# A Trainium2 kernel of two transformer layers: the convolution's input blocks turned on VectorE and through DRAM instead of on TensorE

## The chip, the core and the metric

The kernel is one program on one core of a Trainium2 chip. The metric is the device time of one execution in microseconds (us), the median of several. A core has TensorE (matmuls, whose results land in eight PSUM banks), VectorE (DVE), ScalarE (ACT), GpSimd (POOL) and SyncE (SP, which here issues nearly all DMAs), each with an instruction queue of its own that runs in order; they wait for each other on semaphores.

## The reference

Two transformer layers in sequence on an activation of 256 tokens by 1024 features, all in float32. The first has two kinds of attention and an MLP. The second has a gated FFN (ffn1), a mixing part (mix) and another gated FFN (ffn2). The change is in the mixing part, whose projection `z` is cut into the inputs of two branches; the first 1024 columns of `z` go through a causal convolution of width 4 over the tokens, channel by channel:

```python
u = rms_norm(x, mix_norm_g) * (1 + sc2) + sh2
z = u @ w_mix + b_mix
...
qk_m = jax.nn.silu(causal_conv(jnp.concatenate([q_m, k_m], axis=-1), conv_w, conv_b))
q_m, k_m = jnp.split(qk_m, 2, axis=-1)
h_m = mlstm_chunkwise(...)            # needs q_m and k_m of every channel
y_a = sigmoid(o_m) * rms_norm(h_m, mlstm_norm_g)
y_b = forgetting_attention(q_f, k_f, v_f, f_f, ...)   # "fox" in the kernel, 16 heads
merged = sigmoid(g_a) * (y_a @ w_branch_a) + sigmoid(g_b) * (y_b @ w_branch_b)
x = x + g2 * (merged @ w_out)
```

## The kernel before

**Matmuls.** Every projection is cut into blocks of 512 output columns (`conv0`, `conv1`, `vm0`, ...), a block into units of two k tiles of 128 rows, a unit into two halves, one for each row tile of 128 tokens. A raw float32 weight unit of 512 KB is loaded by SP (L2692), ScalarE rounds it to its high half `whi` (L1595), VectorE subtracts to get the low half `wlo` (L1983), and TensorE makes three float32r matmuls of 512 columns for each k tile and half: high by high, low by high, high by low (L1319, L1323, L1324). There are four raw buffers and five pairs of whi and wlo. SP loads the raw of a unit once the wlo of an earlier one has freed its buffer.

**The order.** A planner in Python (`plan`) writes one list, `order`, that all five engines walk through; each issues the entries that concern it. Everything besides the matmuls is a *job*: a generator with segments. After each half (and once more after each block) the planner ticks; a job whose lag has run down puts its next segment into the list, at most three jobs a tick. The lags between segments are the numbers of the table `LAG`, by kind and segment. Jobs take and drop buffers (`Ring`): four natural buffers `nat`, four PSUM banks `misc`, two convolution buffers `zp`, one `blocked_h` and one `land_h`. A `drain` ticks without halves until a job is done.

The blocks of the mixing part come as conv0, the small block gate, conv1, vm0, vm1, fox0 to fox3 (queries and keys of the fox attention), fv0, fv1, o0, o1, ga0, ga1, ba0 and on. conv0 ends at half 330 of the list, conv1 at 338, vm0 at 346, vm1 at 354, fox0 at 362, fox1 at 370, fox2 at 378, fox3 at 386, fv0 at 394, fv1 at 402, o0 at 410, o1 at 418, ga0 at 426.

**The convolution.** A block's two row tiles lie in PSUM with tokens on the partitions; the convolution wants channels there. ScalarE copies the tiles to `nat` (L1857). TensorE turns them by 128x128 transposes against an identity into a `misc` bank (L1518), four for each of two parts. ScalarE adds the bias and writes `zp` (L1868), VectorE makes the four taps into `qkT` (L2425, L2428), ScalarE applies Silu (L1875). In the list: the copy after half 330 (conv0) and 338 (conv1); conv0's four tap segments after halves 332, 338, 346 and 353, conv1's after 341, 347, 355 and 362; the last Silu after 359 and 368.

**What follows.** `mlstm` starts when conv0, conv1, vm0, vm1 and `gates` are done, here after half 377: for each of four heads one segment of scores (L1533) and two of sums (L1544 to L1547), with a VectorE normalisation each (L2477 to L2483) and a square on ScalarE (L1888); its last segment, the mean (L2488), stands after half 409. Behind block o0 the plan drains mlstm. Then SP loads `NF`, the forget terms of the fox attention (`load_nf`, L2808, two loads of 1 MB that wait for mlstm's last square and put), GpSimd masks them (L2627), and the first fox softmax (`fx0s`, L2205 on VectorE, L1754 on ScalarE) comes after half 418, ten ticks after fox3 is done and o0 has ended. The first turn of its results on TensorE (L1439) comes after half 423. The power on GpSimd that o0's normalisation (L2531) needs is L2594.

**The fox heads** already go the way that the change gives to the convolution: VectorE turns 32x32 blocks of two natural tiles into `blocked_h` (L2509), SP writes it to a DRAM scratch and reads it back into `land_h` in four pieces that put the blocks in place (`shuttle_heads`, L2731 and L2738), and ScalarE takes it from there (L1904). `land_h` has one buffer, so one block at a time is on this way.

Of the kernel before, what the change touches and what calls it, by code (L numbers as in the profile page):

```python
# [32 lines left out]
       ("attn_bw", 0): 2, ("attn_bw", 1): 6, ("attn_bw", 2): 1, ("attn_bw", 3): 24, ("conv", 0): 1, ("conv", 1): 2,  # L33
       ("conv", 2): 7, ("end", "late"): 6, ("end", "lead"): 4, ("ffn1", "between0"): 0, ("ffn1", "between1"): 0,
# [3 lines left out]
       ("fox", "fetch"): 6, ("fox", "put"): 4, ("gate", "ga0"): 15, ("gate", "ga1"): 24, ("gate", "gb0"): 8,  # L38
       ("gate", "gb1"): 11, ("fox", 0): 2, ("fox", 1): 5, ("fox", 2): 5, ("fx0", "wait"): 15, ("fx0s", "round"): 15,
# [8 lines left out]
       ("gates", 0): 11, ("gates", 1): 5, ("gates", 2): 20, ("gates", 3): 10, ("gates", 4): 6, ("glu", "fetch"): 4,  # L48
       ("glu", "upper"): 10, ("glu", "lower"): 0, ("glu", 0): 3, ("heads", "turn"): 3, ("heads", 0): 3,
       ("heads", 1): 3, ("heads", 2): 2, ("mT", "turn"): 0, ("mT", "wait"): 5, ("mix", "between0"): 0,  # L50
       ("mix", "between1"): 0, ("mix", "hold0"): 1, ("mix", "hold1"): 0, ("mix", "late"): 5, ("mix", "lead"): 5,
       ("mix", "turn0"): 3, ("mix", "turn1"): 2, ("mlp", "between0"): 0, ("mlp", "between1"): 0, ("mlp", "hold0"): 0,
       ("mlp", "hold1"): 0, ("mlp", "late"): 2, ("mlp", "turn0"): 3, ("mlp", "turn1"): 1, ("mlstm", 0): 4,
       ("mlstm", 1): 1, ("mlstm", 2): 4, ("o", 0): 1, ("o", 1): 5, ("o", 2): 18, ("pace", "gb0"): 4,
# [95 lines left out]
def build(nc, d, out):  # L150
# [3 lines left out]
    ACT = mybir.ActivationFunctionType  # L154
# [328 lines left out]
    def plan():  # L483
# [818 lines left out]
    def tensor_program(pe):  # L1302
# [207 lines left out]
        def conv_job(name):  # L1510
            yield
            for p in range(2):
                bank = misc.buf(name, p)
                pe.wait_ge(*misc.free(name, p))
                pe.wait_ge(*conv_in(name, 1))
                for c in range(2):
                    for t in range(2):
                        r = pe.e.transpose(bank[:, c * 256 + t * 128:c * 256 + t * 128 + 128],  # L1518
                                           nat.buf(name, t)[:, (2 * p + c) * 128:(2 * p + c + 1) * 128], ident[:, :])
                r.then_inc(turned.up(name, p), 1)  # L1520
                for _ in range(3):
                    yield
            for t in range(2):
                nat.give(turned(name, 1), name, t)
            yield

# [27 lines left out]
        def mT_job(c):  # L1554
# [6 lines left out]
                "conv0": conv_job("conv0"), "conv1": conv_job("conv1"), "mT0": mT_job(0), "mT1": mT_job(1)}  # L1561
# [28 lines left out]
    def scalar_program(act):  # L1590
# [262 lines left out]
        def conv_job(name, c0):  # L1853
# [6 lines left out]
            yield  # L1860
            for p in range(3):
                if p < 2:
                    z, bank = zp.buf(name, p), misc.buf(name, p)
                    act.wait_ge(*turned(name, p))
                    act.wait_ge(*zp.free(name, p))
                    act.wait_ge(*zero_zp(1))
                    for c in range(2):
                        r = act.e.activation(z[:, c, 3:259], bank[:, c * 256:(c + 1) * 256], ACT.Identity,  # L1868
                                             bias=col("bqk", c0 + 2 * p + c))
                    r.then_inc(conv_bias.up(name, p), 1)  # L1870
                    misc.give(conv_bias(name, p), name, p)
# [100 lines left out]
    def vector_program(dve):  # L1972
# [442 lines left out]

        def conv_job(name, c0):
            yield
# [73 lines left out]
        def fox_qk_job(name):  # L2491
# [12 lines left out]
            dve.wait_ge(*blocked_h.free(name))  # L2504
            dve.wait_ge(*gated("mix", 1, 1))
            o = blocked_h.buf(name)[:, :].rearrange("p (b t c j) -> p t b c j", b=4, t=2, c=4)
            for t in range(2):
                dve.wait_ge(*hn_out(name, t))
                v.transpose(o[:, t], bufs[t][:, :].rearrange("p (c b i) -> p b c i", c=4, b=4)).then_inc(  # L2509
                    swapped.up(name, t), 1)  # L2510
                nat.give(swapped(name, t), name, t)
# [171 lines left out]
    def sync_program(sp):  # L2683
# [41 lines left out]
        def shuttle_heads(name):  # L2725
            a = 262144
            for _ in range(3):
                yield
# [228 lines left out]
```

## Time and profile before

| | |
|---|---|
| time, median of 3 runs | 945.15 us (944.3 to 945.33) |
| time of the profiled execution | 944.73 us |
| its span | 943.4 us |
| TensorE busy | 935.1 us, 99% |
| VectorE busy | 718.6 us, 76% |
| ScalarE busy | 509.9 us, 54% |
| GpSimd busy | 50.1 us, 5% |
| DMA, mean over the span | 255 GB/s |
| TensorE's granted clock | 0.999 of full speed |

The span is that of the instructions in the trace; the time of the same execution is 1.3 us longer. Busy time of TensorE counts a matmul from its issue to its end, and matmuls overlap: of the 512 column matmuls a new one starts every 0.23 us though each lasts 0.39. What a piece of work costs TensorE is thus read from start times in a timeline and not from durations. A share of 76% for VectorE is a mean over the whole span; stretches stand higher.

### The profile page before, as it was taken

Reading aid. Unit: us, or ns where it says so; the run is one execution under the profiler, and the core shown is the slowest. Engines: PE = TensorE matmul, PEld = TensorE weight load, DVE = VectorE, ACT = ScalarE, POOL = GpSimd, SP = SyncE. Lnnn points to the kernel's source line nnn. Section 1 sums busy time; section 2 is a strip of 40 time slices with the busy share of each in tenths; the row PEclk is TensorE's granted clock in tenths of the full one; section 3 lists DMA queues with packets and bytes.
Section 4 is the critical chain, followed back from the end, with each engine's and each line's share of the span. In section 5 each row is a group of like instructions: output and inputs, shape, how many; then the busy total and the mean of one; then the engine's idle time right before and its main releaser. Section 6 shows DMA issues by size and latency. Waiting matters only on the chain.

```text
span 943.4 us, 12244 instructions
## 1 busy us (share of the span) xinstructions
PE 935.1 (99%) x4426; PEld 772.3 (82%) x4426; DVE 718.6 (76%) x1090; ACT 509.9 (54%) x792; POOL 50.1 (5%) x58
## 2 busy tenths in 40 slices
PE   9999999999999999999999999999999999999998
PEld 7878788888887888888888888878788888888886
DVE  6897689998676888777769999788666765566662
ACT  6686665564446445454576565456464574544440
POOL 2410000000000000000000121110000000000000
PEclk9999999999999999999999999999999999999999
DMA  9840779999894989998747889984735647666870
GB/s 341 266 152 23 246 245 372 389 387 371 286 317 148 332 326 343 320 345 299 274 133 259 279 281 283 302 338 147 234 125 188 213 137 264 225 223 223 300 234 23
DMA packets 123130, 240.31 MB, mean 255 GB/s; under 512 B 9346, under 2 KB 28954, under 8 KB 122814
## 3 DMA queue, kind: packets, MB, share of 16 engines
q1 hardware_dynamic: 122926, 239.27, 73.8%
q8 instruction: 35, 0.57, 0.2%
q10 hardware_dynamic: 144, 0.27, 0.1%
q14 instruction: 25, 0.20, 0.1%
HBM read 226.35 MB, written 14.20 MB: 255 GB/s over the span
## 4 chain that ended last, share of the span: by engine, by line
PE 87%; DVE 5%; DMA 5%; ACT 1%; issue 1%; SPq 1%; POOL 0%; DVEq 0%; ACTq 0%
PE ps L1319 27%; PE ps L1324 26%; PE ps L1323 26%; DMA raw<-in_w_mix 2%; DVE wlo L1983 2%; PE ps L1458 2%; PE ps L1414 1%; PE ps L1439 1%; PE ps L1350 1%; DMA land_h<-scr_u 1%; PE ps L1372 1%; ACT whi L1595 1%; DMA raw<-in_w_up 1%; DMA raw<-in_w_in 1%; PE ps L1571 1%
## 5 line engine op out<-in xcount | busy, mean ns | idle before, releaser
L1595 ACT ACTIVATE whi<-raw 128x1024 fp32r<-128x1024 f32 (+1 forms) x285 | 294.5, 1046 | 272.6 <-PE ps L1324 169.5
L1983 DVE TENSOR_TENSOR wlo<-raw,whi 128x1024 fp32r<-128x1024 f32 (+1 forms) x285 | 338.4, 1203 | 106.3 <-ACT whi L1595 105.8
L1319 PE MATMUL ps<-whi,hTh 128*128 128x512 f32 (+1 forms) x760 | 300.0, 395 | 0.2 <-DVE nat L2129 0.2
L1324 PE MATMUL ps<-whi,hTl 128*128 128x512 f32 (+1 forms) x760 | 294.4, 387 | 0.0
L1323 PE MATMUL ps<-wlo,hTh 128*128 128x512 f32 (+1 forms) x760 | 294.3, 387 | 0.0
L1319 PEld LDWEIGHTS ps<-whi,hTh 128*128 128x128 f32 x760 | 142.9, 188 | 30.8 <-issue 2.5
L1324 PEld LDWEIGHTS ps<-whi,hTl 128*128 128x128 f32 x760 | 142.7, 188 | 29.5
L1323 PEld LDWEIGHTS ps<-wlo,hTh 128*128 128x128 f32 x760 | 142.9, 188 | 27.8
L2325 DVE CUSTOM_DVE_ANT_0 araw<-araw,crow,colp 128x1024 f32<-128x1024 f32 x72 | 91.9, 1277 | 0.1
L2594 POOL TENSOR_TENSOR stat<-stat,mhalf 128x8 f32<-128x8 f32 (+3 forms) x29 | 36.2, 1260 | 586.0 <-DVE stat L1999 460.3
L1319 PE MATMUL ps<-whi,uh_ffn 128*128 128x512 f32 x164 | 63.9, 390 | 0.0
L1324 PE MATMUL ps<-whi,ul_ffn 128*128 128x512 f32 x164 | 63.8, 389 | 0.0
L1323 PE MATMUL ps<-wlo,uh_ffn 128*128 128x512 f32 x164 | 63.8, 389 | 0.0
L1319 PE MATMUL ps<-whi,uh 128*128 128x512 f32 x128 | 49.9, 390 | 0.0
L1323 PE MATMUL ps<-wlo,uh 128*128 128x512 f32 x128 | 49.8, 389 | 0.0
L1324 PE MATMUL ps<-whi,ul 128*128 128x512 f32 x128 | 49.8, 389 | 0.0
L2374 DVE TENSOR_TENSOR nat<-ps,nat 128x512 f32<-128x512 f32 (+1 forms) x24 | 15.4, 646 | 29.7 <-PE ps L1324 22.3
L1319 PEld LDWEIGHTS ps<-whi,uh_ffn 128*128 128x128 f32 x164 | 30.8, 188 | 6.4
L1324 PEld LDWEIGHTS ps<-whi,ul_ffn 128*128 128x128 f32 x164 | 30.8, 188 | 6.4
L1323 PEld LDWEIGHTS ps<-wlo,uh_ffn 128*128 128x128 f32 x164 | 30.8, 188 | 6.3
L1324 PEld LDWEIGHTS ps<-whi,ul 128*128 128x128 f32 x128 | 24.0, 188 | 5.0
L1323 PEld LDWEIGHTS ps<-wlo,uh 128*128 128x128 f32 x128 | 24.0, 188 | 5.0
(276 smaller groups left out, 1129.2 us busy)
## 6 DMA issues: line engine op xcount, KB each, us to landing
raw<-in_ffn_w_in SPq DMA_DIRECT2D x80, 512.0 KB, 5.1
araw<-in_w_mod SPq DMA_DIRECT2D x72, 512.0 KB, 5.6
raw<-in_w_mix SPq DMA_DIRECT2D x64, 512.0 KB, 4.9
raw<-in_ffn_w_out SPq DMA_DIRECT2D x44, 512.0 KB, 4.9
raw<-in_w_up SPq DMA_DIRECT2D x32, 512.0 KB, 5.4
raw<-in_w_down SPq DMA_DIRECT2D x32, 512.0 KB, 5.3
scr_u<-blocked SPq DMA_DIRECT2D x18, 512.0 KB, 5.0
raw<-in_w_out SPq DMA_DIRECT2D x16, 512.0 KB, 4.3
```

Source lines behind the costliest of these rows:

```text
L1319: pe.e.matmul(o, ah, h[:, j, :], start=s0, stop=False, skip_group_check=True)
L1323: pe.e.matmul(o, ah, l[:, j, :], start=False, stop=False, skip_group_check=True)
L1324: r = pe.e.matmul(o, al, h[:, j, :], start=False, stop=s1, skip_group_check=True)
L1350: r = pe.e.transpose(bank[:, c * 128:(c + 1) * 128], src[:, (4 * p + c) * 128:(4 * p + c + 1) * 128], ident[:, :])
L1372: r = pe.e.transpose(bank[:, c * 256 + t * 128:c * 256 + t * 128 + 128], src[t][:, (2 * p + c) * 128:(2 * p + c + 1) * 128], ident[:, :])
L1414: return pe.e.matmul(bank[:, c * w:(c + 1) * w], Q[rows, hp + c, ts], K[rows, kc(c), 0:w], start=True, stop=True)
L1458: r = pe.e.matmul(ob[:, h * 64:(h + 1) * 64], buf[:, (nk * c + k) * 128:(nk * c + k + 1) * 128], (fV if a["fox"] else VA)[:, k, v0:v0 + 64 ...
L1595: act.e.activation(uflat(whi, u), uflat(raw, u), ACT.Copy).then_inc(hi.up(u), 1)
L1983: v.tensor_tensor(uflat(wlo, u), uflat(raw, u), uflat(whi, u).bitcast(f32), SUB).then_inc(lo_dve.up(u), 1)
L2325: v.tensor_tensor_reduce(out=w, in0=w, in1=crow[:, :], scale=1.0, scalar=col("bada", 8 * m + i), op0=MUL, op1=ADD, accum_out=to).then_inc( ...
L2374: v.tensor_tensor(b[:, 0:n], pair_of(key)[t][:, c:512], b[:, 0:n], MUL).then_inc(glu.up(name, t), 1)
L2594: g.tensor_tensor(o, a, mhalf[:, 0:n], ALU.pow).then_inc(rstd.up(*key), 1)
```

## The change

In `job_conv` the planner no longer takes a `misc` bank; after the copy it waits until `blocked_h` and `land_h` are free, takes both, and has three new steps: the swap, the fetch (lag 6) and the put (lag 4). TensorE's `conv_job` is gone. VectorE makes the same block transposes as for the fox heads, by a helper `swap_heads` that both use. SP runs `shuttle_heads` for conv0 and conv1 too. ScalarE's bias activations read `land_h` instead of PSUM. The lags of several jobs are changed with it: conv 0 (1 to 2), fox fetch (6 to 4), fox put (4 to 6), fox 1 (5 to 9), fox 2 (5 to 1), fx0s wait (10 to 8), fx0s 0 to 3 (3, 4, 22, 2 to 11, 1, 14, 9), gates 1 (5 to 1), gates 3 (10 to 9), mlstm 2 (4 to 1), o 2 (18 to 15). All others stay.

```diff
@@ plan: job_conv
             yield lag("conv", 0, 2)
+            while None not in blocked_h.held or None not in land_h.held:
+                yield 1
+            blocked_h.take(name)
+            land_h.take(name)
+            seg(name)
+            blocked_h.drop(name)
+            natural_end(name)
+            yield lag("conv", "fetch", 6)
+            seg(name)
+            yield lag("conv", "put", 4)
             for p in range(2):
                 if p:
                     zp.drop(name, p - 1)
-                misc.take(name, p)
                 zp.take(name, p)
                 seg(name)
-                misc.drop(name, p)
+                if p:
+                    land_h.drop(name)
                 yield lag("conv", 1, 2)
...
             zp.drop(name, 1)
             seg(name)
-            natural_end(name)
@@ TensorE
-        def conv_job(name):
-            yield
-            for p in range(2):
-                bank = misc.buf(name, p)
-                pe.wait_ge(*misc.free(name, p))
-                pe.wait_ge(*conv_in(name, 1))
-                for c in range(2):
-                    for t in range(2):
-                        r = pe.e.transpose(bank[:, c * 256 + t * 128:c * 256 + t * 128 + 128],
-                                           nat.buf(name, t)[:, (2 * p + c) * 128:(2 * p + c + 1) * 128], ident[:, :])
-                r.then_inc(turned.up(name, p), 1)
...
@@ ScalarE: conv_job
+            view = land_h.buf(name)[:, :].rearrange("p (a t c j) -> p c t a j", a=4, t=2, c=4)
...
-                    z, bank = zp.buf(name, p), misc.buf(name, p)
-                    act.wait_ge(*turned(name, p))
+                    z = zp.buf(name, p)
+                    act.wait_ge(*ld_h(name, 3))
...
-                        r = act.e.activation(z[:, c, 3:259], bank[:, c * 256:(c + 1) * 256], ACT.Identity,
-                                             bias=col("bqk", c0 + 2 * p + c))
+                        r = act.e.activation(z[:, c, 3:259].rearrange("p (t a j) -> p t a j", t=2, a=4), view[:, 2 * p + c],
+                                             ACT.Identity, bias=col("bqk", c0 + 2 * p + c))
...
@@ VectorE
+        def swap_heads(name, ready):
+            dve.wait_ge(*blocked_h.free(name))
+            dve.wait_ge(*gated("mix", 1, 1))
+            o = blocked_h.buf(name)[:, :].rearrange("p (b t c j) -> p t b c j", b=4, t=2, c=4)
+            for t in range(2):
+                dve.wait_ge(*ready(name, t))
+                v.transpose(o[:, t], nat.buf(name, t)[:, :].rearrange("p (c b i) -> p b c i", c=4, b=4)).then_inc(
+                    swapped.up(name, t), 1)
+                nat.give(swapped(name, t), name, t)
+
         def conv_job(name, c0):
+            yield
+            swap_heads(name, conv_in)
+            yield
             yield
@@ SP
         def shuttle_heads(name):
             a = 262144
-            for _ in range(3):
+            for _ in range(1 if name[:4] == "conv" else 3):
                 yield
...
+        for c in range(2):
+            jobs[f"conv{c}"] = shuttle_heads(f"conv{c}")
```

## Rows read from the trace of the kernel before

**Rows 1.** The page: busy us, share of the span and instructions of each engine.

```profile
PE 935.1 (99%) x4426; PEld 772.3 (82%) x4426; DVE 718.6 (76%) x1090; ACT 509.9 (54%) x792; POOL 50.1 (5%) x58
```

**Rows 2.** Busy time by stretches of the span; last columns granted clock, DMA share, GB/s.

```profile
core 0: us, PE busy (x) PEld busy (x) DVE busy (x) ACT busy (x) POOL busy (x), PEclk, DMA share, GB/s
...
500.00:520.00 20.00, 20.00 (x95) 16.45 (x94) 19.02 (x30) 11.90 (x15) 1.41 (x2) 1.00 0.72 244
...
600.00:620.00 20.00, 20.00 (x92) 16.12 (x91) 16.46 (x27) 9.33 (x16) 3.72 (x2) 1.00 1.02 337
```

**Rows 3.** Timelines of VectorE and TensorE near 638 us: start, duration, engine, line.

```profile
636.24 2.10 DVE L1983 TENSOR_TENSOR wlo<-raw,whi 128x1024 fp32r<-128x1024 f32 x1
...
639.65 0.48 PE L1319 MATMUL ps<-whi,hTh 128*128 128x512 f32 x1
```

**Rows 4.** Timelines of TensorE and ScalarE near 625 us; in brackets idle time and releaser.

```profile
626.60 0.63 PE L1439 MATMUL ps<-ident,fP 128*128 128x128 f32 x4 [0.71 <-ACT fP L1754]
...
624.41 1.06 ACT L1595 ACTIVATE whi<-raw 128x1024 fp32r<-128x1024 f32 x1 [7.07 <-DMA raw<-in_w_mix]
```

**Rows 5.** Timeline of TensorE round the second group of transposes.

```profile
499.71 0.39 PE L1323 MATMUL ps<-wlo,hTh 128*128 128x512 f32 x1
499.94 0.40 PE L1324 MATMUL ps<-whi,hTl 128*128 128x512 f32 x1
500.18 0.60 PE L1518 MATMUL ps<-ident,nat 128*128 128x128 f32 x4
...
500.86 0.39 PE L1323 MATMUL ps<-wlo,hTh 128*128 128x512 f32 x1
```

**Rows 6.** The fox heads' landing buffer: ScalarE's waits and landings; then DMA issues.

```profile
  DMA land_h<-scr_u: 7.5, 3
...
DMA to landing us min/median/max: 3.9/6.0/7.4
...
scr_u<-gate SPq DMA_DIRECT2D x4, 512.0 KB, 3.4
```

**Rows 7.** VectorE: the fox transposes; timelines of three taps, of an mlstm normalisation.

```profile
L2509 DVE STREAM_TRANSPOSE gate<-nat x8: 665/684/706, 548.7 to 593.0; 128x512 f32<-128x512 f32 x8
...
498.43 1.53 DVE L2428 SCALAR_TENSOR_TENSOR qkT<-zp,colp,qkT 128x256 f32<-128x256 f32 x3
...
600.75 0.21 DVE L2477 TENSOR_SCALAR stat<-ps,emt 128x1 f32<-128x1 f32 x1
...
601.38 0.48 DVE L2483 TENSOR_SCALAR W<-ps,stat 128x256 f32<-128x256 f32 x1
```

**Rows 8.** Timeline of TensorE round one sum of mlstm.

```profile
558.65 0.59 PE L1544 MATMUL ps<-Vm,fP 128*128 128x257 f32 x2
558.89 0.58 PE L1319 MATMUL ps<-whi,hTh 128*128 128x512 f32 x1
```

**Rows 9.** conv1's last Silu on ScalarE, and TensorE's matmul behind half 368.

```profile
540.15 0.61 ACT L1875 ACTIVATE qkT<-qkT 128x512 f32<-128x512 f32 x1
...
541.64 0.39 PE L1319 MATMUL ps<-whi,hTh 128*128 128x512 f32 x1
```

**Rows 10.** The loads of NF, GpSimd's power and mask, and VectorE's wait for it.

```profile
L2808 SPq DMA_DIRECT2D NF<-scr_g x2: 419/428/437, 607.0 to 607.5; - x2
...
DMA to landing us min/median/max: 11.6/12.7/13.7
...
605.50 2.54 POOL L2594 TENSOR_TENSOR stat<-stat,mhalf 128x8 f32<-128x8 f32 x1 [26.93 <-DVE stat L2488]
618.83 2.09 POOL L2627 TENSOR_SCALAR_AFFINE_SELECT NF<-NF 128x1024 f32<-128x1024 f32 x1 [10.79 <-DMA NF<-scr_g]
...
621.06 0.42 DVE L2205 CUSTOM_DVE_ANT_0 fP<-ps,NF 128x256 f32<-128x256 f32 x1 [1.10 <-POOL NF L2627]
```

**Rows 11.** Timeline of TensorE: the first matmuls of o1 and of ga0's third unit.

```profile
606.76 0.39 PE L1319 MATMUL ps<-whi,hTh 128*128 128x512 f32 x1
...
624.37 0.39 PE L1319 MATMUL ps<-whi,hTh 128*128 128x512 f32 x1
```

More of the change, by code:

```diff
@@ L32 @@
        ("attn_bt", 0): 6, ("attn_bt", 1): 1, ("attn_bt", 2): 4, ("attn_bt", 3): 10, ("attn_bw", "round"): 10,
-       ("attn_bw", 0): 2, ("attn_bw", 1): 6, ("attn_bw", 2): 1, ("attn_bw", 3): 24, ("conv", 0): 1, ("conv", 1): 2,
+       ("attn_bw", 0): 2, ("attn_bw", 1): 6, ("attn_bw", 2): 1, ("attn_bw", 3): 24, ("conv", 0): 2, ("conv", 1): 2,
        ("conv", 2): 7, ("end", "late"): 6, ("end", "lead"): 4, ("ffn1", "between0"): 0, ("ffn1", "between1"): 0,
        ("ffn1", "hold0"): 0, ("ffn1", "hold1"): 0, ("ffn1", "late"): 3, ("ffn1", "lead"): 4, ("ffn1", "turn0"): 3,
[2 rows of a table removed]
@@ L38 @@
-       ("fox", "fetch"): 6, ("fox", "put"): 4, ("gate", "ga0"): 15, ("gate", "ga1"): 24, ("gate", "gb0"): 8,
-       ("gate", "gb1"): 11, ("fox", 0): 2, ("fox", 1): 5, ("fox", 2): 5, ("fx0", "wait"): 15, ("fx0s", "round"): 15,
[8 rows of a table removed]
-       ("gates", 0): 11, ("gates", 1): 5, ("gates", 2): 20, ("gates", 3): 10, ("gates", 4): 6, ("glu", "fetch"): 4,
-       ("glu", "upper"): 10, ("glu", "lower"): 0, ("glu", 0): 3, ("heads", "turn"): 3, ("heads", 0): 3,
-       ("heads", 1): 3, ("heads", 2): 2, ("mT", "turn"): 0, ("mT", "wait"): 5, ("mix", "between0"): 0,
@@ L51 @@
[L51 to L54, printed above, removed]
[2 rows of a table added]
+       ("fox", "turn"): 3, ("fox", "fetch"): 4, ("fox", "put"): 6, ("gate", "ga0"): 15, ("gate", "ga1"): 24,
@@ new lines @@
+       ("gate", "gb0"): 8, ("gate", "gb1"): 11, ("fox", 0): 2, ("fox", 1): 9, ("fox", 2): 1, ("fx0", "wait"): 15,
[8 rows of a table added]
+       ("fx1w", 6): 5, ("fx1w", 7): 1, ("gates", 0): 11, ("gates", 1): 1, ("gates", 2): 20, ("gates", 3): 9,
+       ("gates", 4): 6, ("glu", "fetch"): 4, ("glu", "upper"): 10, ("glu", "lower"): 0, ("glu", 0): 3,
+       ("heads", "turn"): 3, ("heads", 0): 3, ("heads", 1): 3, ("heads", 2): 2, ("mT", "turn"): 0, ("mT", "wait"): 5,
+       ("mix", "between0"): 0, ("mix", "between1"): 0, ("mix", "hold0"): 1, ("mix", "hold1"): 0, ("mix", "late"): 5,
@@ L55 @@
+       ("mix", "lead"): 5, ("mix", "turn0"): 3, ("mix", "turn1"): 2, ("mlp", "between0"): 0, ("mlp", "between1"): 0,
+       ("mlp", "hold0"): 0, ("mlp", "hold1"): 0, ("mlp", "late"): 2, ("mlp", "turn0"): 3, ("mlp", "turn1"): 1,
+       ("mlstm", 0): 4, ("mlstm", 1): 1, ("mlstm", 2): 1, ("o", 0): 1, ("o", 1): 5, ("o", 2): 15, ("pace", "gb0"): 4,
        ("pace", "gb1"): 9, ("pace", "kb"): 1, ("pace", "ob0"): 6, ("pace", "ob1"): 16, ("pace", "qa"): 11,
@@ L59 @@
        ("ta", "turn"): 1, ("ta", "wait"): 19, ("u", "fetch"): 6, ("u", "upper"): 10, ("u", "lower"): 1, ("u", 0): 3,
[1 row of a table removed]
+       ("vb", 0): 2, ("yT", "turn"): 24, ("yb", "turn"): 14, ("yb", "wait"): 9, ("conv", "fetch"): 6,
+       ("conv", "put"): 4}
 ROUNDS = (("soft", 0), ("soft", 1), ("mix", 0), ("soft", 2), ("mix", 1), ("soft", 3), ("mix", 2), ("mix", 3))
@@ L1508, in gates_job @@
                 yield
-        def conv_job(name):
-            yield
-            for p in range(2):
-                bank = misc.buf(name, p)
-                pe.wait_ge(*misc.free(name, p))
-                pe.wait_ge(*conv_in(name, 1))
-                for c in range(2):
-                    for t in range(2):
-                        r = pe.e.transpose(bank[:, c * 256 + t * 128:c * 256 + t * 128 + 128],
-                                           nat.buf(name, t)[:, (2 * p + c) * 128:(2 * p + c + 1) * 128], ident[:, :])
-                r.then_inc(turned.up(name, p), 1)
-                for _ in range(3):
[L1522 to L1525, printed above, removed]
         def mlstm():
@@ L1560, in tensor_program @@
                 "yb0": turns("yb0", 2, lambda t: yb_put(0, t)), "yb1": turns("yb1", 2, lambda t: yb_put(1, t)),
-                "conv0": conv_job("conv0"), "conv1": conv_job("conv1"), "mT0": mT_job(0), "mT1": mT_job(1)}
+                "mT0": mT_job(0), "mT1": mT_job(1)}
         for name in ("qb", "kb"):
@@ L1867, in conv_job @@
                     for c in range(2):
-                        r = act.e.activation(z[:, c, 3:259], bank[:, c * 256:(c + 1) * 256], ACT.Identity,
-                                             bias=col("bqk", c0 + 2 * p + c))
+                        r = act.e.activation(z[:, c, 3:259].rearrange("p (t a j) -> p t a j", t=2, a=4), view[:, 2 * p + c],
+                                             ACT.Identity, bias=col("bqk", c0 + 2 * p + c))
                     r.then_inc(conv_bias.up(name, p), 1)
-                    misc.give(conv_bias(name, p), name, p)
+                    if p:
+                        land_h.give(conv_bias(name, p), name)
                 if p:
@@ L2414, in gates_job @@
                 yield
+        def swap_heads(name, ready):
[7 more added lines that the diff above has]
+                nat.give(swapped(name, t), name, t)
         def conv_job(name, c0):
+            yield
+            swap_heads(name, conv_in)
+            yield
             yield
@@ L2503, in fox_qk_job @@
             yield
[L2504 to L2511, printed above, removed]
+            swap_heads(name, hn_out)
             yield
@@ L2726, in shuttle_heads @@
             a = 262144
-            for _ in range(3):
+            for _ in range(1 if name[:4] == "conv" else 3):
                 yield
```

21 rows, old and new, of the table LAG are left out of this document.

## The prediction

> **What bounds the kernel.** I read the page's busy times first: TensorE shows 935.1 us of a 943.4 us span [rows 1], so the time is TensorE's, and the table of stretches shows it busy without a break from 480 to 620 us, where the changed work lies [rows 2]. The same table shows VectorE at 19.02 of 20 us there and the DMA engines at 0.72 to 1.02: whatever leaves TensorE goes to two resources with little left. The kernel gains only what leaves TensorE, and loses wherever VectorE hands over a weight's low half (wlo) later than TensorE wants it. That margin is small at places: one wlo ends at 638.34 and its first matmul starts at 639.65 [rows 3]. From 500 to 700 us the one plain wait of TensorE is 0.71 us at 626.60, for ScalarE [rows 4].
>
> **What is removed.** Sixteen transposes in four groups of four. In the timeline [rows 5] the matmul before a group starts at 499.94 and the second matmul behind it at 500.86: 0.92 us where two ordinary steps take 2 x 0.227 (499.71 to 499.94 is one). A group therefore costs 0.47 us: its issue and about 0.09 us on the first matmul behind it. Four make 1.9 us (1.7 if the group that the small gate transposes follow saves less, since those stay). The row gives 0.60 us from the first start to the last end of a group; 4 x 0.60 = 2.4 us is the upper bound, which the start times exclude, since the next matmul begins before the last one ends. The Trainium skill (VectorE: DVE Perf Modes, Rules for kernel authors) speaks against the change: for a full 128x128 transpose use TensorE if a PSUM destination is fine, since VectorE turns 32x32 blocks only. By its table of bf16 transposes (390 ns on TensorE) the 16 would be an estimated 6.2 us; the rows give 1.9.
>
> ScalarE's eight bias activations read SBUF instead of PSUM: nothing, since ScalarE has slack (11.90 busy of 20 us).
>
> **What is added.** Four VectorE block transposes of 684 ns [rows 7], 2.7 us, and two trips through DRAM: one 512 KB write and four 128 KB reads each, 10 DMA issues on SP's queue, 2 MB in all. For the fox heads the write lands in 3.4 us and a read in 3.9 to 7.4 [rows 6]. Nothing on TensorE waits for the trips themselves: the next reader is ScalarE, and behind it in its queue are the whi conversions, which now and then wait up to about 3 us more for a landing, as they did for the fox heads (7.5 us in three waits [rows 6], with no gap on TensorE). SP waits for the swap with raw loads queued behind, but for the same VectorE that those loads wait for.
>
> The 2.7 us on VectorE are covered by what is moved. The order counts a tick after each half (two k tiles of one row tile, 12 matmuls a unit of two halves, 2.74 us) and one more after each block. By LAG, conv0's swap comes at half 331, its taps at 341, 347, 355 and 361 (before: 332, 338, 346, 353). There is one landing buffer, so conv1 cannot swap until conv0 gives it up at half 354; its taps come at 365, 371, 379 and 385, and it ends at half 392 instead of 368. A tap segment is 1.9 us: three taps of 1.53 us together behind a first one [rows 7]. VectorE's work done up to a given half is thus below before until about half 400, by up to 5 us. The gate scans come one tick before TensorE's gate transposes instead of five; by the relieved VectorE queue they still end some 1 us earlier: priced at 0 (up to 1 us without that relief).
>
> **What is late next.** mlstm starts when conv1 is done: half 392, not 377. With the lag 4 cut to 1 it takes 24 ticks instead of 36, and the plan drains it behind block o0 (half 410). It used to end at 409; now its last four ticks fall into the drain, where no half lies between them. Three consequences.
>
> First, three float32 groups of TensorE stand side by side. A lone one costs the first matmul behind it extra time: behind the one at 558.65, of 0.24 us, the next matmul shows 0.58 us instead of 0.39 [rows 8]. Two such edges in the drain, and one where a double tick joins two groups, are worth about 0.4 us (0 to 0.6).
>
> Second, mlstm's first scores follow conv1's last Silu in the same tick. Before, that Silu ended at 540.76 and TensorE came to its place at 541.64 [rows 9]. I add 0.4 us (0 if it is as early again, 1.5 if ScalarE sits in a DMA wait).
>
> Third, the loads of NF (the forget terms) wait on SP for mlstm's last squares. Call P the time at which TensorE starts block o1; before, it was 606.76, and NF was issued at 607.0, landed in 11.6 us, and GpSimd's mask ended at 620.92, P + 14.2 [rows 10]. The first fox softmax on VectorE needs the mask and waited 1.10 us for it. Now at P come the last two steps on VectorE (two times 1.1 us [rows 7]), ScalarE's square and the mean, with hand-overs some 3.8 us: NF goes out at P + 3.8. With the same queueing the mask ends at P + 17.4; with an emptier queue (a landing of 7 us, which is the longest of a 0.1 MB read) at P + 12.8. And the softmax is placed earlier: fox3 is done at tick 95, the lag is 8 instead of 10, so it stands at half 416 and not 418, ahead of the wlo of the third unit of ga0. VectorE is in order: softmax 1.5 us, the two steps of o0 (1.3 us) and that wlo (1.2 us) follow the mask, so the wlo ends between P + 16.8 and P + 21.4. TensorE wants it at 624.37, P + 17.6 [rows 11]. Stall: 0 to 3.8 us. The power on GpSimd (2.54 us) also moves from before P to P + 6.3 [rows 10], o0's normalisation waits for it, and the wlo behind that ends near P + 9.2 where it is wanted at P + 8.2: about 1 us, part of the same loss. I take 2.3 us for both, nearer the middle, since the DMA engines are full there (1.02 [rows 2]).
>
> In return the 0.71 us wait of rows 4 goes: it came because the exponentials stood behind a whi that waited 7.07 us for its raw, and two halves earlier they stand ahead of it. The margin between that softmax and the first turn grows from five halves to seven.
>
> **Sum.** Against the profiled execution's own 944.73 us (span 943.4 and 1.3 around it): -1.9 - 0.4 - 0.7 + 0.4 + 2.3 = -0.3, so 944.4. The median of the runs shown is 945.15, 0.4 above the profiled one; I forecast 944.5. A measurement of this kernel tells about 0.2% (1.9 us) from no change.
>
> **The rivals.**
> - *Same* (forecast, 0.42): the removed 3.0 us are mostly given back at the NF wait. 943.3 to 946.9; its own range 943.4 to 946.4.
> - *The full gain* (0.30): NF lands early, or VectorE comes to the softmax late anyway, as with the 1.10 us before. Then 944.73 - 3.0 + 0 to 1.1 = 941.7 to 942.8 in the profiled time, 942.2 to 943.2 as a median. For it: TensorE has not one wait in 500 to 620 us, so every removed cycle counts. Against it: the placement of the softmax, which the lags fix.
> - *VectorE becomes the bound behind the late mlstm* (slower, 0.20): place, halves 410 to 420; the mask at P + 17.4, and the weights behind it (each later raw waits on SP for an earlier wlo, and lands after 5 us or, as the one that ScalarE waited 7.07 us for, much later) miss their time too. It decides once the wlo end more than 5 us late. 944.73 - 3.0 + 6 to 7 = 947.7 to 948.7; with a softmax turn caught as well, 949.
> - *The landing is the loss* (slower, 0.08): a read of conv's blocks lands late in the busy DMA (7.4 us and more), and ScalarE holds back the whi behind it for longer than margins like that of rows 3 allow, once for each of the two blocks, 2 to 3 us each: 944.7 - 3.0 + 5 = 946.7 to 947.5.
> - That the transposes were hidden and nothing is saved: the start times of rows 5 exclude it.
>
> **Range and chances.** No gain beyond 3.0 us exists, so 942.2 is the floor; the upper end takes in the first 1.5 us of the slower cases: 942.2 to 947.5 leaves out about 2 in 10. Faster by over 0.2%: 0.30, within: 0.42, slower: 0.28.
>
> **What would show it.** In the profile after: no L1518 groups, first matmuls of blocks spaced 0.23 us at those places; L2509's line in its helper with 12 instead of 8 transposes; a wait of VectorE's softmax on GpSimd's NF mask of 3 to 5 us instead of 1.10; a gap on TensorE at the third unit of ga0 behind wlo, and perhaps at the fourth of o1; no wait on fP at the first fox turn; a short wait at mlstm's first scores. I am wrong if the NF wait is no longer than before (full gain) or if TensorE has gaps between halves 340 and 390 (the trips or the queue of VectorE cost something there).

## The result and the profile after

The changed kernel takes 950.86 us (median of 4 runs, 949.63 to 952.36) against 945.24 for the kernel before (4 runs, 944.3 to 945.79): ratio 1.0057, 95% interval 1.0035 to 1.0079. It is slower by 5.6 us, outside the forecast range. The profiled execution took 952.36 us, the longest of the four, with a span of 951.0 us, 7.6 above that of before, so the balance below is that of a run 1.5 us over the median.

The page's busy times after, to be laid beside [rows 1]:

```profile
PE 935.6 (98%) x4410; PEld 770.4 (81%) x4410; DVE 720.2 (76%) x1094; ACT 514.6 (54%) x795; POOL 48.3 (5%) x58
```

Sixteen matmul instructions fewer, and TensorE's busy time is no smaller. The stretches show where the idle time came in (columns as in [rows 2]):

```profile
500.00:520.00 20.00, 20.00 (x92) 16.33 (x91) 14.32 (x23) 7.91 (x10) 1.42 (x2) 1.00 0.79 251
520.00:540.00 20.00, 20.00 (x90) 16.57 (x89) 19.04 (x29) 11.04 (x13) 1.23 (x1) 1.00 1.00 327
540.00:560.00 20.00, 17.13 (x75) 13.58 (x74) 17.54 (x27) 18.52 (x27) 5.37 (x4) 1.00 0.68 224
560.00:580.00 20.00, 16.94 (x73) 13.05 (x71) 19.72 (x33) 11.44 (x17) 3.41 (x2) 1.00 0.95 310
580.00:600.00 20.00, 19.30 (x81) 16.07 (x82) 19.01 (x35) 8.76 (x17) 3.33 (x2) 0.91 0.89 281
```

From 500 to 520 us VectorE is busy for 14.32 us where it had 19.02 [rows 2]. Behind that, TensorE loses about 6.6 us between 540 and 600. Its timeline gives the gaps, each with its length and releaser in brackets:

```profile
545.43 0.47 PE L1329 MATMUL ps<-whi,hTh 128*128 128x512 f32 x1 [2.41 <-DVE wlo L1980]
557.05 0.47 PE L1329 MATMUL ps<-whi,hTh 128*128 128x512 f32 x1 [0.46 <-DVE wlo L1980]
565.84 0.50 PE L1329 MATMUL ps<-whi,hTh 128*128 128x512 f32 x1 [0.36 <-DVE wlo L1980]
569.87 0.47 PE L1329 MATMUL ps<-whi,hTh 128*128 128x512 f32 x1 [0.99 <-DVE wlo L1980]
580.70 0.67 PE L1526 MATMUL ps<-qkT 128*128 128x256 f32 x2 [2.40 <-ACT qkT L1872]
```

Four gaps are waits for a weight's low half, 4.2 us; the fifth is mlstm's first scores behind conv1's last Silu, 2.40 us. Right behind the fifth the granted clock falls to half, as a window laid on that place shows, and the starts of the matmuls move from 0.23 us apart to 0.43:

```profile
581.40:584.80 3.40, 3.40 (x10) 2.71 (x9) 3.40 (x4) 1.06 (x1) 2.63 (x2) 0.50 0.53 156
585.00:590.00 5.00, 5.00 (x24) 4.17 (x23) 4.81 (x10) 2.13 (x5) 0.00 (x0) 1.00 1.07 329
```

```profile
582.75 0.63 PE L1329 MATMUL ps<-whi,hTh 128*128 128x512 f32 x1
583.17 0.63 PE L1333 MATMUL ps<-wlo,hTh 128*128 128x512 f32 x1
...
585.08 0.39 PE L1329 MATMUL ps<-whi,hTh 128*128 128x512 f32 x1
585.31 0.39 PE L1333 MATMUL ps<-wlo,hTh 128*128 128x512 f32 x1
```

That stretch at the 1.2 GHz level lasts 3.4 us and costs half of it, 1.7 us. The balance of the profiled run: gaps +6.6, clock +1.7, transposes -1.9, the wait of rows 4 -0.7, and 0.4 that was there before the first conv: +6.1 of 7.6. The other 1.5 us are spread over the float32 groups that moved and the first matmuls behind gaps, and I give them to no row.

The 2.41 us gap can be followed back. First ScalarE, then VectorE:

```profile
541.23 0.91 ACT L1864 ACTIVATE zp<-land_h,colp 128x256 f32<-128x256 f32 x2 [2.86 <-DMA land_h<-scr_u]
```

```profile
542.17 0.41 DVE L2435 TENSOR_SCALAR qkT<-zp,colp 128x256 f32<-128x256 f32 x1 [2.69 <-ACT zp L1864]
542.62 1.53 DVE L2438 SCALAR_TENSOR_TENSOR qkT<-zp,colp,qkT 128x256 f32<-128x256 f32 x3
544.07 2.36 DVE L1980 TENSOR_TENSOR wlo<-raw,whi 128x1024 fp32r<-128x1024 f32 x2
```

conv1's block lands late, ScalarE waits for it, VectorE stands with its taps for 2.69 us, and the wlo behind the taps come late to TensorE. The trace has a second, earlier chain. SP's DMA issues (start, time of the issue), then ScalarE:

```profile
497.00 2.68 SPq L2741 DMA_DIRECT2D land_h<-scr_u  x4
499.72 0.43 SPq L2695 DMA_DIRECT2D raw<-in_w_mix  x1
...
501.99 0.31 SPq L2798 DMA_DIRECT2D scr_g<-F  x1
509.34 0.38 SPq L2800 DMA_DIRECT2D EM<-scr_g  x1
...
510.32 1.01 SPq L2695 DMA_DIRECT2D raw<-in_w_mix  x2
```

```profile
506.36 0.91 ACT L1864 ACTIVATE zp<-land_h,colp 128x256 f32<-128x256 f32 x2 [5.83 <-DMA land_h<-scr_u]
...
517.49 1.06 ACT L1588 ACTIVATE whi<-raw 128x1024 fp32r<-128x1024 f32 x1 [5.85 <-DMA raw<-in_w_mix]
```

The 20 KB store of the gate rows goes out at 501.99, behind conv0's reads. SP waits 7.0 us for it before it may read those rows back, with the raw loads queued behind; before, the same wait was 1.6 us. Not all of the growth is the trip's: with the new lags alone (e2_lags below) the wait is 3.1 us. The Trainium skill (DMA: Bandwidth & Descriptors, Anatomy of one DMA — SWDGE (gpsimd) path) gives a DMA on GpSimd's path a fixed cost of about 2.0 us. This store is issued by SP; its wait of before is near that figure, and that of after is far over it. These two chains, VectorE's load, the lags, and the single landing buffer were then set against each other.

### The profile page after: what moved, and what is told of

It is laid out like the page before. It is cut to its first block, busy times and chain, and to the rows that moved or that the text cites. A ratio compares the mean times of both kernels' runs of the same rounds, so it can differ in the third digit from the quotient of the medians.

```text
span 951.0 us, 12233 instructions
## 1 busy us (share of the span) xinstructions
PE 935.6 (98%) x4410; PEld 770.4 (81%) x4410; DVE 720.2 (76%) x1094; ACT 514.6 (54%) x795; POOL 48.3 (5%) x58
## 4 chain that ended last, share of the span: by engine, by line
PE 85%; DVE 7%; DMA 4%; ACT 2%; issue 2%; SPq 0%; POOL 0%; DVEq 0%; ACTq 0%
PE ps L1329 26%; PE ps L1333 26%; PE ps L1334 26%; DVE wlo L1980 3%; PE ps L1468 2%; DMA land_h<-scr_u 1%; ACT whi L1588 1%; PE ps L1424 1%; PE ps L1382 1%; PE ps L1449 1%; DMA raw<-in_w_mix 1%; PE ps L1360 1%; DVE araw L2322 1%; DMA raw<-in_w_up 1%; DMA raw<-in_ffn_w_in 1%
## 5 line engine op out<-in xcount | busy, mean ns | idle before, releaser
L2597 POOL TENSOR_TENSOR stat<-stat,mhalf 128x8 f32<-128x8 f32 (+3 forms) x29 | 34.1, 1188 | 594.4 <-DVE stat L1996 461.0
L1329 PEld LDWEIGHTS ps<-whi,uh 128*128 128x128 f32 x128 | 24.0, 188 | 5.0
```

What stands on the lines that cost most here:

```text
L1329: pe.e.matmul(o, ah, h[:, j, :], start=s0, stop=False, skip_group_check=True)
L2597: g.tensor_tensor(o, a, mhalf[:, 0:n], ALU.pow).then_inc(rstd.up(*key), 1)
```

## The experiments

Each kernel's ratio is to the kernel before in the same series of runs. Fourteen kernels were run. A ratio has an interval of 0.1 to 0.2% to each side, 1 us or more, and several steps below are no larger. So a second measure stands beside it. Every trace holds the same 3696 matmuls of 512 columns, and from the start of the 1801st to that of the 2521st (in the kernel before from 460.69 to 651.13 us) each covers the changed work and leaves out what varies ahead of it; behind this piece no two of the kernels below drift apart by more than 0.1 us. What a kernel takes there beyond the kernel before is called its *excess* below; it comes from one execution each and has no interval. For the changed kernel it is 7.2 us, 1.7 of it the half clock.

**e1_notrans.** The kernel before without TensorE's transposes; ScalarE reads natural instead of turned blocks, which leaves the transposition out of the result.

```diff
-                "conv0": conv_job("conv0"), "conv1": conv_job("conv1"), "mT0": mT_job(0), "mT1": mT_job(1)}
+                "mT0": mT_job(0), "mT1": mT_job(1)}
...
-                    act.wait_ge(*turned(name, p))
+                    act.wait_ge(*conv_in(name, 1))
```

> The kernel before, with the sixteen transposes on TensorE left out: ScalarE's bias activations read the natural tiles as they are, so the convolution runs on untransposed data (that part of the computation is changed). Nothing else moves. It measures the price of the transposes by itself. By the start times of the timeline they are worth 1.9 us: 943.3 us, ratio 0.998. If their whole durations counted it would be 4.4 us: 940.8. If they were hidden: 945.2.

Measured: 942.73 us, ratio 0.9982 (0.9972 to 0.9991), so -1.7 us. The first term of the forecast, 1.9, stands: over the transposes the trace gains 1.9 us. Its excess is -2.6, since the 0.71 us wait of [rows 4] is gone here too, although no lag was changed.

**e2_lags.** The kernel before with the new lags of all other jobs (fox, fx0s, gates, mlstm, o).

```diff
+LAG.update({('fox', 'fetch'): 4, ('fox', 'put'): 6, ('fox', 1): 9, ('fox', 2): 1, ('fx0s', 'wait'): 8,
...
```

> The kernel before, transposes on TensorE and all, with the changed lags of fox, fx0s, gates, mlstm and o alone (conv's own lag stays at 1). If the loss of 5.6 us comes from the landing way (one buffer, late landings, mlstm late), this one stays within 1.5 us of before, 943.7 to 946.7. If it comes from the retuned lags of the other jobs, it is as slow as the changed kernel: 948 to 951.

Measured: 945.37 us, ratio 1.0005 (0.9996 to 1.0014). The lags alone cost nothing that can be told (excess -0.15).

**e3_two.** The changed kernel with a second blocked buffer, landing buffer and DRAM block for conv1, and the lags of the other jobs as before, so that conv1 need not wait for conv0.

```diff
-    blocked_h = Ring([gates[0]])
+    blocked_h, blocked_c = Ring([gates[0]]), Ring([gates[1]])
+    land_c = Ring([W1[:, 1, :]])
```

> The changed kernel with a second way for conv1: its blocks go into the other gate row's tile, through a DRAM slot of their own and land in the upper half of W1, so that conv1 need not wait for conv0's landing buffer. All lags of the other jobs as before the change; conv's are 2, fetch 4, put 6, last 6, so that conv1's last Silu stands after half 374 and mlstm starts at 377 as before. If the single landing buffer and what it makes late is the cause, the 1.9 us of the transposes are kept: 943.0 to 944.0. If the cause is VectorE's 2.7 us of swaps, or the trips as such, it stays slow: 948 to 951.

Measured: 955.3 us, ratio 1.011 (1.0095 to 1.0124): by the ratios 5 us worse than the changed kernel. TensorE's waits:

```profile
PE ps L1533 <- ACT qkT L1880: 4.2, 1, 4.2
PE ps L1336 <- DVE wlo L1988: 2.6, 3, 1.1
```

A second landing buffer does not bring the gain back. Since the two trips and the taps also stand closer together here, and the waits are more, this run does not price the buffer by itself.

**e4_noland.** The changed kernel, but conv's bias activations read a weight tile (W1) and wait for no landing; swaps and trips are all done.

```diff
-            view = land_h.buf(name)[:, :].rearrange("p (a t c j) -> p c t a j", a=4, t=2, c=4)
+            view = W1[:, 0, :].rearrange("p (a t c j) -> p c t a j", a=4, t=2, c=4)
...
-                    act.wait_ge(*ld_h(name, 3))
```

> The changed kernel with swaps, writes and reads in their places, but ScalarE's bias activations of the convolution read a tile that is already there (a half of W1) and so wait for no landing; the convolution's data are changed by it. If ScalarE's wait for conv1's landing is what holds VectorE's taps and the wlo behind them, the gap of 2.41 us at 545 us and those behind it go, with the wait of 2.40 us for the last Silu left: 946 to 948.5. If VectorE is simply overfull, nothing changes: 950 to 951.

Measured: 948.14 us, ratio 1.0038 (1.0026 to 1.0051). TensorE's waits in its trace:

```profile
PE ps L1526 <- ACT qkT L1871: 2.4, 1, 2.4
PE ps L1329 <- DVE wlo L1979: 2.3, 4, 1.0
```

The long gap of 2.41 us is gone, but four waits for wlo stay and most of the loss with them. The landing wait is worth 1.8 us by the ratios (their intervals overlap), about a third. By the excesses, 7.2 and 3.3, it is 3.9, of which 1.7 are the half clock that this execution did not have.

**e5_gatewait.** The changed kernel with SP's wait for the gate rows' store and the loads behind it a segment later.

```diff
+LAG.update({('gates', 1): 6, ('gates', 2): 15})
...
             q.dma_start(scrG[4:24, :], F8[:, :]).then_inc(st_gates.up(1), 16)
+            yield
             sp.wait_ge(*st_gates(1))
```

> The changed kernel; on SP the wait for the landing of the gate rows in DRAM, and the two EM loads behind it, stand one segment later (lags gates 1 = 6, gates 2 = 15, so that the later gate segments keep their places). In the changed kernel SP stood 7.0 us in that wait with raw loads queued behind it, 1.6 us before the change. If that queueing is a main cause, VectorE gets its raws earlier and the wlo waits of TensorE (4.2 us in four) shrink: 947 to 949. If it is not: 950 to 951.

Measured: 949.82 us, ratio 1.0058 (1.0045 to 1.0071); TensorE waits 2.4 us in 4 for wlo and 2.4 for the Silu. The wlo waits shrink by 1.8 us as forecast, the time does not: with the landing wait in place the stand of SP makes no difference in it that can be told. The excess, 5.2, is 2.0 better, but it is one execution.

**e6_spread.** The changed kernel with the landing given more time (lag put 8 instead of 4), conv's last lag shortened, and mlstm at its old place.

```diff
+LAG.update({('conv', 'put'): 8, ('conv', 2): 5})
...
+            yield 4
```

> The changed kernel with conv's put lag 8 instead of 4 and its last lag 5 instead of 7: ScalarE asks for a landing four ticks later, the buffer is given up at the same tick as before, the last Silu of conv1 stands four ticks earlier, and mlstm still starts at its old place. ScalarE's waits for the two landings (8.7 us) and TensorE's 2.40 us wait for the Silu should go; the SP wait stays. Theory landing and Silu: 945.5 to 947.5. Theory VectorE overfull: the wlo waits stay, 948.5 to 950.

Measured: 952.84 us, ratio 1.0091 (1.0078 to 1.0104). ScalarE waits for no landing of conv; wlo are late for 4.9 us in 4 waits, up to 2.4. More time for the landing does not help. That this is so because the taps move further into a stretch where VectorE is full fits the wlo waits, but was not tested.

**e7_both.** The edits of e5_gatewait and e6_spread together:

```diff
+LAG.update({('gates', 1): 6, ('gates', 2): 15, ('conv', 'put'): 8, ('conv', 2): 5})
...
+            yield 4
...
+            yield
             sp.wait_ge(*st_gates(1))
```

> The two edits together: SP's wait one segment later, landings asked for later, Silu four ticks ahead of mlstm. If waits in line (landing, SP, Silu) are the whole loss, the gain of the transposes comes out: 943 to 944.5. What stays above that is the price of VectorE's 2.7 us of swaps and of the late mlstm: 945 to 948.

Measured: 948.93 us, ratio 1.0052 (1.004 to 1.0064): 3.9 us better than e6_spread. So here SP's stand did cost; wlo still 3.8 us in 4.

**e8_silu.** The changed kernel with mlstm two ticks later, so that TensorE would not meet the Silu:

```diff
+            yield 2
```

> The changed kernel with mlstm two ticks later behind conv1's last Silu, nothing else. TensorE's wait of 2.40 us there should go, and the half clock behind it, if that comes from the gap. Theory Silu: 947 to 949. If the time is only moved to the late end of mlstm (VectorE and SP behind it): 950 to 951.

Measured: 952.69 us, ratio 1.0085 (1.0071 to 1.0098). The Silu wait is gone and wlo come late for 7.1 us in 7 waits, up to 3.2. So the 2.4 us cannot simply be subtracted: where this edit takes them away, as much or more is paid elsewhere. The edit also makes mlstm later still, and which of the two brings the new waits stays open.

**e9_noswap and e10_empty.** From e4_noland first VectorE's swaps are taken away (the trips carry the buffer as it is), then the trips too. What stays of the change in e10_empty is the places and the missing transposes.

```diff
-            swap_heads(name, conv_in)
+            for t in range(2):
+                nat.give(conv_in(name, t), name, t)
```

```diff
-        for c in range(2):
-            jobs[f"conv{c}"] = shuttle_heads(f"conv{c}")
```

> The version without the landing wait (e4_noland), with VectorE's four swaps of the convolution's blocks left out as well: the DMA trips stay and carry the buffer as it is. VectorE is given back 2.7 us, 1.3 of it between 540 and 560 us. Theory VectorE is too full there: the waits of TensorE's matmuls for wlo (four, up to 2.3 us in e4_noland) shrink to under 1 us in all and the median is 945 to 946.3 us. Theory the cost is where the work stands or what the DMA queues carry, not the swaps: 947.5 to 948.5 us, as e4_noland (948.14).

> As e9_noswap, and the DMA trips of the convolution are left out too: what is left of the change is that the 16 TensorE transposes are gone and that the convolution's and the mLSTM's pieces stand at their new places. Beside e1_notrans (942.73, same pieces at the old places) it prices the places alone. Theory places cost (taps moved into a full stretch): at least 944.5 us, 2 us or more over e1_notrans. Theory swaps and trips are the whole cost: 942.5 to 943.5 us. What the trips themselves cost is its difference from e9_noswap; if the queues do not matter, under 0.5 us.

Measured: e9_noswap 947.47 us, ratio 1.0033 (1.002 to 1.0045); e10_empty 944.39 us, ratio 0.9998 (0.9989 to 1.0006). I had expected the large step at the swaps. By the ratios it is at the trips, whose landing nothing on ScalarE waits for in either kernel: without swaps the time is that of e4_noland within the interval; without trips it falls by 3.1 us, and there the intervals are apart. The excesses (e4_noland 3.3, e9_noswap 1.6, e10_empty 0.0) give the trips 1.6 and the swaps 1.7. Both measures say that the trips cost something; only the ratios say that they cost more than the swaps. The chain shows in the waits of SP and ScalarE and in VectorE's timeline, first of e9_noswap:

```profile
SPq L2800 <- DMA scr_g<-F: 6.5, 1, 6.5
```

```profile
516.67 1.06 ACT L1588 ACTIVATE whi<-raw 128x1024 fp32r<-128x1024 f32 x1 [6.65 <-DMA raw<-in_w_mix]
```

```profile
517.77 2.50 DVE L1979 TENSOR_TENSOR wlo<-raw,whi 128x1024 fp32r<-128x1024 f32 x2 [3.11 <-ACT whi L1588]
```

and of e10_empty, SP and ScalarE at the same places:

```profile
SPq L2800 <- DMA scr_g<-F: 3.1, 1, 3.1
```

```profile
511.25 1.06 ACT L1588 ACTIVATE whi<-raw 128x1024 fp32r<-128x1024 f32 x1 [3.62 <-DMA raw<-in_w_mix]
```

With the trips the raws land late, and VectorE stands idle for 3.11 us with wlo, right ahead of the 20 us from 520 us in which it has under one to spare. TensorE's waits in e10_empty are smaller:

```profile
PE ps L1526 <- ACT qkT L1871: 1.6, 1, 1.6
...
PE ps L1329 <- DVE wlo L1979: 0.4, 1, 0.4
```

The profiled spans are 945.9 and 942.6. Of the 3.3 us between them 1.6 arise ahead of the first conv, where the kernels do the same; 1.6 are the waits of the Silu (2.4 against 1.6) and of wlo (1.2 against 0.4). The medians, 3.1 apart over 12 runs each, hold a part that the profiled pair lacks: in 10 of e9_noswap's 12 runs the mean granted clock was under 1.000 (0.996 to 0.999), in e10_empty's 6 of 12 (all 0.999), in e2_lags' none of 11. The two e9_noswap runs at 1.000 average 945.3 us and the six at 0.998 948.3. A run at 0.998 has lost about 0.002 x 946 = 1.9 us to the clock, about as much as the piece at half clock at 581 us above. Over all 12 runs the mean clock is 0.9984 against 0.9995, an estimated 1.0 of the 3.1 us. So about a third of what the trips cost by the ratios is granted clock; that the trips' waits bring this about is not shown.

Beside e1_notrans (0.9982) e10_empty prices the places and, with them, the new lags of the other jobs: +1.5 us, less than the 2 that I had put to it; the intervals overlap by 0.0002, and e2_lags gave 0.5 for the lags alone (its interval takes in 0). By the excesses it is 2.6. In the trace 2.0 of them are two waits of TensorE: 1.6 for conv1's last Silu and 0.4 for a wlo.

**e11_half.** The kernel before with conv0 alone sent by swaps and trip, the swap put where VectorE had been idle, conv1 turned by TensorE.

```diff
+            far = name == "conv0"
...
+                if not far:
+                    misc.take(name, p)
...
+        jobs["conv0"] = shuttle_heads("conv0")
```

> Only conv0's block goes by VectorE's swaps and the DRAM trip, placed where VectorE stood idle before the gate matmuls; conv1's block is turned by TensorE as before, and every other job keeps its place. TensorE saves 8 transposes (0.9 us). Theory VectorE room: the stretch from 520 us on is left alone, no wlo wait over 1 us appears, and the median is 943.3 to 944.2 us, a little faster than before. Theory any trip costs more than the transposes: 945.5 us or more.

Measured: 944.7 us, ratio 0.9999 (0.9989 to 1.0008). No wait for wlo and a full VectorE:

```profile
500.00:520.00 20.00, 20.00 (x94) 16.36 (x93) 19.07 (x31) 12.23 (x17) 1.42 (x2) 1.00 0.84 287
520.00:540.00 20.00, 20.00 (x92) 16.55 (x91) 19.50 (x35) 10.45 (x14) 0.80 (x1) 1.00 0.82 265
```

Placed so, a trip makes no wlo late, but the 0.9 us that its 8 transposes should give is not seen in the time (the excess, -0.6, has it in part), and the result is neither of my two ranges. No version of the idea that was run beats the kernel before.

**e12_landgate, e13_trip1, e14_trip0.** How do the trips cost 3 us? e12_landgate is e4_noland with the edit of e5_gatewait:

```diff
+LAG.update({('gates', 1): 6, ('gates', 2): 15})
...
+            yield
             sp.wait_ge(*st_gates(1))
```

The other two are e9_noswap with one trip each:

```diff
-        for c in range(2):
-            jobs[f"conv{c}"] = shuttle_heads(f"conv{c}")
+        jobs["conv1"] = shuttle_heads("conv1")
```

(`conv0` for e14_trip0).

> The version without the landing wait (e4_noland: the bias activations read W1 instead of the landed block), and in it the gate jobs' pieces one segment later as in e5_gatewait, so that SP does not stand for the gate rows' tiny store with raw loads behind it. Theory the trips cost because SP stands 7 us behind them: 945 to 946.3 us, no ScalarE wait for a raw load over 4 us between 500 and 520 us. Theory the trips cost by what they carry on the queue, or the places cost: 947.5 to 948.5 us, as e4_noland (948.14).

> As e9_noswap (no swaps by VectorE, bias activations read W1), and conv0's DMA trip is left out, so that only conv1's is left. e9_noswap with both trips took 3.1 us more than e10_empty with none (947.47 against 944.39). Theory the first trip is the cost, as it stands right ahead of the gate rows' store and the raw loads of 500 to 520 us: 944.4 to 945.2 us. Theory each trip costs the same: about 945.9 us. Theory the second is the cost (it meets the stretch where VectorE is full): 946.8 to 947.5 us.

> The other half of e13_trip1: conv1's DMA trip is left out and conv0's is left. Theory the first trip is the cost: 946.8 to 947.5 us, with SP's wait for the gate rows' store at 6 us or more and a ScalarE wait for a raw load over 5 us, as in e9_noswap. Theory each trip costs the same: about 945.9 us. Theory the second is the cost: 944.4 to 945.2 us.

Measured: e12_landgate 946.92 us, ratio 1.0022 (1.0012 to 1.0033); e13_trip1, with conv1's trip, 944.92, ratio 1.0 (0.9989 to 1.0012); e14_trip0, with conv0's, 946.61, ratio 1.0013 (1.0005 to 1.0022). SP's wait and ScalarE's longest wait with the first trip alone (e14_trip0):

```profile
SPq L2800 <- DMA scr_g<-F: 5.9, 1, 5.9
```

```profile
517.01 1.06 ACT L1588 ACTIVATE whi<-raw 128x1024 fp32r<-128x1024 f32 x1 [7.06 <-DMA raw<-in_w_mix]
```

and with the second alone (e13_trip1):

```profile
SPq L2800 <- DMA scr_g<-F: 2.8, 1, 2.8
```

```profile
512.24 1.06 ACT L1588 ACTIVATE whi<-raw 128x1024 fp32r<-128x1024 f32 x1 [3.78 <-DMA raw<-in_w_mix]
```

The first trip makes the gate rows' store and the raws late, and the second does not; that much the rows show. What each costs is not shown. By the ratios the first costs 1.4 us, the second alone 0.2 and both 3.3, but the intervals of the two single trips overlap (1.0005 to 1.0022, 0.9989 to 1.0012). Their traces do not part them: the excesses are 0.8 and 0.7, about the 1.6 of both together, and TensorE's waits are the same in each, 2.4 us for the Silu and 0.4 for one wlo. In e14_trip0 7 of 11 runs had a mean clock of 0.998, in e13_trip1 4 of 12 were at 0.998 or lower; the runs at 1.000 average 945.3 and 944.7 us. So by the traces SP's stand is not the only way in which a trip costs: the second has its excess of 0.7 us without it. Taking the stand away gives back 1.5 us (e12_landgate against e4_noland), with intervals that overlap by 0.0007.

## Why the prediction was wrong

The ladder of ratios, from the kernel before at 1:

| kernel | ratio | what it adds to the one above | us | excess, and its step |
|---|---|---|---|---|
| e1_notrans | 0.9982 | transposes gone | -1.7 | -2.6, -2.6 |
| e10_empty | 0.9998 | the new places and lags | +1.5 | 0.0, +2.6 |
| e9_noswap | 1.0033 | the DMA trips | +3.3 | 1.6, +1.6 |
| e4_noland | 1.0038 | VectorE's four swaps | +0.5 | 3.3, +1.7 |
| changed | 1.0057 | ScalarE's wait for the landing | +1.8 | 7.2, +3.9 (1.7 of it clock) |

Steps need not add up in another order. Of the last four only the step of the trips has intervals that are apart, and the two measures rank the four differently, so which part is the largest stays open. That the four together turn a gain of 1.7 us into a loss of 5.4 is shown.

**The step that failed** is "Nothing on TensorE waits for the trips themselves". I looked at who reads the landed block and at SP's wait for the swap, and left out what the ten new issues do to the transfers queued behind them. In e9_noswap no computing engine waits for the trips, and yet they cost 3.3 us by the ratios (about 1.0 of it clock), 1.6 in the traces. What the traces show of the way: conv0's trip stands ahead of raws and of a 20 KB store on which SP waits; that store kept SP for 5.7 to 7.2 us instead of 2.8 to 3.1 with the new lags and no conv0 trip, and the raws behind it, then whi, then wlo came late. How conv1's trip costs was not followed. I had the parts: the landing times of [rows 6] and the DMA share of [rows 2]. ScalarE's wait for the landing was priced at nothing in the sum, at up to 3 us without a gap; it was 5.83 and 2.86 us, the second with a gap of 2.41 us. The rival "the landing is the loss" had this second mechanism with 0.08; by e4_noland it is 1.8 of 5.6 us, with intervals that overlap.

**The second failed step** is that "VectorE's work done up to a given half is thus below before until about half 400", read as cover. The places were right: the taps come at halves 341 to 361 and 365 to 385, as worked out from LAG. But work that is later is not room gained. What VectorE did not do from 500 to 520 us became idle time (5.7 us of it), since wlo cannot be made ahead of its raw; the taps then met 20 us in which it already worked 19.6, as the row of the kernel before shows:

```profile
520.00:540.00 20.00, 20.00 (x91) 16.54 (x91) 19.61 (x32) 12.30 (x15) 1.62 (x2) 1.00 0.86 297
```

The +1.5 of e10_empty fits this only in part: from 560 to 580 us its VectorE works 19.8 of 20 us, but of TensorE's waits there 1.6 us are for the Silu and 0.4 for a wlo. That this lost time on VectorE is what made the trips' lateness cost is argued, not shown.

**The Silu term** had the right place and the wrong size: 0.4 (0 to 1.5) against 2.40 in the trace. In e10_empty, without swaps, trips and landing wait, it is still 1.6, so most of it comes with the new places: there the Silu stands on ScalarE behind squares that waited 1.17 us for VectorE and two whi. By e8_silu it cannot be taken away by moving mlstm alone.

**The NF term** of 2.3 us, which decided the forecast, did not come. NF went out at 616.9, landed in 7.8 to 10.1 us, and the mask (1.10 us from 624.82) was done 2.2 us ahead of VectorE's first softmax:

```profile
617.12 1.64 POOL L2597 TENSOR_TENSOR stat<-stat,mhalf 128x8 f32<-128x8 f32 x1 [33.09 <-DVE stat L2498]
624.82 1.10 POOL L2630 TENSOR_SCALAR_AFFINE_SELECT NF<-NF 128x1024 f32<-128x1024 f32 x1 [6.06 <-DMA NF<-scr_g]
```

```profile
628.13 0.41 DVE L2202 CUSTOM_DVE_ANT_0 fP<-ps,NF 128x256 f32<-128x256 f32 x1
```

Block o1 starts at P = 614.6 here, so the mask ended at P + 11.3 (forecast P + 12.8 to P + 17.4). VectorE, late itself, came after it, and behind 580.70 us the trace shows no wait of TensorE up to 700. The saving of 0.4 us for float32 groups that stand together was measured by no run.

**Right** were the 1.9 us of the transposes (1.7) and the end of the wait of [rows 4], though the reason given was not needed for it: the wait is gone in e1_notrans as well, where the exponentials keep their place in the list. The swaps, held to be covered, cost 0.5 us by the ratios, within the interval, and 1.7 by the excesses: not settled. The rival of a VectorE that becomes the bound names a resource that is part of it and had the time nearest to the measured one (947.7 to 948.7, or 949), but placed it behind mlstm at halves 410 to 420; the gaps lie at halves 371 to 393. The prediction's own test, gaps between halves 340 and 390, named the failure.

## What to carry to other kernels

Before a transfer is added, list what is queued behind it on its DMA queue, above all small stores that the issuing engine waits for, and follow each delay to the engine with the least room; a transfer that nobody waits for can still cost more than the work that it replaces saved (here 3.3 against 1.7 us by the ratios). Idle time cannot be kept for later: work moved out of a place helps only if its engine can take up something else there. Where differences are near the interval of the ratios, lay the same piece of two traces beside them before sizes are ranked. Where several waits show in a row on the bounding engine, take one away to see whether the time falls or the wait only moves.

## What was not expected of the hardware

A gap of 2.40 us on TensorE was followed, 0.7 us after work began again, by 3.4 us at a granted clock of 0.50 (the 1.2 GHz level), with matmul starts 0.43 us apart instead of 0.23; a gap of 2.41 us at 545 us in the same trace was not. e6_spread shows such a piece at 552.7 us, e3_two at 561.3, e12_landgate at 577.1, e5_gatewait at 578.9 and e8_silu at 625.3. The traces of e4_noland, e9_noswap, e13_trip1 and e14_trip0 have the same gap of 2.4 us ahead of mlstm and none behind it. e12_landgate and e8_silu show one more at 72 us each, far from any edit, behind waits that the kernel before has as well without it. So in this kernel a gap of 2.4 us costs 2.4 us in one execution and an estimated 4.1 (2.4 and 1.7) in another; what decides it no run shows. The timed runs of e9_noswap spread by 6.4 us, those of the kernel before in the same series by 3.0, and by 4.5 in the series of e12_landgate to e14_trip0.
